# Decode attention: differential keys transposed by the vector engine in 32x32 blocks and fetched by GpSimd gathers

## The chip, the cores and the metric

The kernel runs on one core of one Trainium2 chip. The metric is the device time of one execution in microseconds (us). The engines are named as in the profile: PE (TensorE, matmuls), DVE (VectorE), ACT (ScalarE), POOL (GpSimd) and SP (SyncE, which here only issues DMAs). A change of 0.2% or more (3.4 us) is what a measurement of this kernel can tell from none.

## The reference, cut to what matters

One decoder layer is computed for a prompt of 512 tokens and for 8 sequences that decode 4 tokens each over 1024 cached tokens. The cache lies in pages of 128 tokens; a page table gives the 8 pages of each sequence. The change touches only the differential attention of the decoding sequences:

```
s_diff = cache_diff_kv[l][page_table].reshape(DB, past_len, 2, DIFF_HEADS, DIFF_DV)
s1 = einsum('bqhd,bkhd->bhqk', q1, k1) * scale + bias      # 8 heads, 64 dims
s2 = einsum('bqhd,bkhd->bhqk', q2, k2) * scale + bias      # the second half of each head
a  = masked_softmax(s1, mask) - lam * masked_softmax(s2, mask)
o  = einsum('bqhk,bkhd->bqhd', a, v)
```

A token has 1024 numbers of keys (8 heads, 2 halves, 64 dims) and 1024 of values, all float32.

## The kernel before, in words

The program has five stages: projections, compression, prompt attention, decode attention, and the closing stage (output projection and MLP). The change lies in decode attention, which runs from about 965 to 1237 us.

Decode attention takes two sequences at a time, in four pairs (i = 0 to 3). `decode_steps` writes the work of all pairs as one list of steps: `cmp` (compressed keys), `sel` (keys of 8 selected-branch pages), `win` (4 window blocks), `dif_n` and `dif` (the new rows and the 8 pages of differential keys, four steps each, m = 0 to 3), then `p_sel`, `p_few`, `p_win` (probabilities times values of the first three branches, "the value steps"), and `p_dif`, `p_dif_n` (probabilities times differential values), which stand in the middle of the next pair, after its sixth `sel` step. Before the change the value steps come after `dif` pages 0 and 1, in the last pair after page 7.

A step has two parts. `turn` makes PE transpose four 128x128 blocks into a PSUM bank, ACT or DVE copies the bank to a slot in SBUF (`owner` says which), and `multiply` makes PE multiply the slot with the queries. PE runs `turn` two steps ahead of `multiply`, and there are four banks and slots. So a page of differential keys costs 16 transposes, 4 copies of 128x512 and 16 score matmuls.

All engines work through the list in order and wait on semaphores. All page loads of this stage are issued by SP, in one order written by hand (`load_v` for differential values, 2 x 512 KB a page for the two sequences; `load_k`/`key_load` for differential keys, the same size; `sel_load`, 2 x 256 KB a page; `win_load`, 2 x 256 KB a block). A load waits for its buffer: values of page k for the `p_dif` matmuls of the pair before; a key page for the turns of the page four before it (there are four key buffers, `KEY_PAGES`); the selected pages of the next pair for all value steps of this one (`nsa_mm`). Key page 0, the selected pages and the windows of pair 0 are loaded during prompt attention.

The compression stage already fetches rows by GpSimd gathers (`page_rows`, L229: 128 rows of 2 KB by an indirect DMA).

## Time and profile before

| | |
|---|---|
| median of 3 runs | 1718.29 us (1717.81 to 1719.01) |
| the profiled execution: its time, its span | 1718.2 us, 1716.4 us |
| mean granted TensorE clock over the span | 0.967 |
| busy, share of the span | PE 93%, DVE 47%, ACT 33%, POOL 11% |
| DMA | 265.67 MB, 155 GB/s in the mean |
| the decode stage | 965.6 us (first DMA issue) to 1236.7 us (its last stores are issued) |

Spans and times of single instructions are from the one profiled execution; 1.8 us of its time lie outside its span. A PE that is shown busy need not be at its peak, and the time of a stage is set by whatever wait ends last in it, not by the busiest engine of the whole span.

### The profile page before, as it was taken

The page shows a single profiled execution, that of the slowest core. Times are in us where ns is not written, and L with a number is a line of the kernel's source. Part 1 is how long each engine was busy: PE and PEld are TensorE (multiplying, and loading weights), DVE is VectorE, ACT ScalarE, POOL GpSimd, SP SyncE. Part 2 cuts the span into 40 slices and gives each one's busy share as a digit, 9 for nine tenths or more (in the row PEclk, how much of TensorE's full clock was granted, in tenths as well). Part 3 has the DMA queues.
Part 4 walks back from the last instruction along what each step waited for, and adds up shares of the span by engine and source line. Part 5 has one row for each costly group of instructions (what it writes and reads, how often), then busy time and mean ns, then how long its engine had stood idle before and what let it go on. Part 6 is the DMA issues. An engine that isn't in the chain of part 4 may idle for free. (4 is left out here: it accounts for less than half of the span.)

```text
span 1716.4 us, 31637 instructions
## 1 busy us (share of the span) xinstructions
PE 1603.7 (93%) x12648; PEld 1329.8 (77%) x12648; DVE 808.1 (47%) x1841; ACT 570.8 (33%) x1185; POOL 180.4 (11%) x269
## 2 busy tenths in 40 slices
PE   6999999998999988799899899889799999999997
PEld 4878888876888875577777776666488999999996
DVE  4576632215443428776766545445355442234322
ACT  4233220223323226656555233233233331133210
POOL 2001000000630000073212000000000000000000
PEclk9999999999999998999999899999899999999998
DMA  8855443434631316344121499998542334334321
GB/s 272 308 172 170 165 139 141 144 84 102 183 105 28 105 38 183 84 173 138 44 77 38 169 386 369 370 347 294 220 143 89 123 103 117 122 99 135 84 73 53
DMA packets 184201, 265.67 MB, mean 155 GB/s; under 512 B 35661, under 2 KB 115917, under 8 KB 183958
## 3 DMA queue, kind: packets, MB, share of 16 engines
q1 hardware_dynamic: 174934, 227.57, 40.4%
q0 software_dynamic: 6016, 25.34, 4.9%
q10 hardware_dynamic: 3136, 11.22, 1.7%
q8 instruction: 73, 1.20, 0.3%
q14 instruction: 42, 0.34, 0.1%
HBM read 241.01 MB, written 42.60 MB: 165 GB/s over the span
## 5 line engine op out<-in xcount | busy, mean ns | idle before, releaser
L648 PE MATMUL pj_ps<-all_hi,pj_xh 128*128 128x512 f32 x480 | 191.7, 399 | 1.5 <-DVE all_lo L536 1.5
L649 PE MATMUL pj_ps<-all_lo,pj_xh 128*128 128x512 f32 x480 | 190.0, 396 | 0.0
L650 PE MATMUL pj_ps<-all_hi,pj_xl 128*128 128x512 f32 x480 | 189.9, 396 | 0.0
L1427 ACT ACTIVATE pa_sc<-pa_sc,pa_nmax 128x32 f32<-128x32 f32 (+4 forms) x256 | 126.0, 493 | 115.7 <-DVE pa_nmax L1476 115.5
L2685 PE MATMUL fi_ps<-fi_fl,fi_wh 128*128 128x272 f32 x512 | 149.2, 291 | 0.0
L2686 PE MATMUL fi_ps<-fi_fh,fi_wl 128*128 128x272 f32 x512 | 148.4, 290 | 0.0
L2684 PE MATMUL fi_ps<-fi_fh,fi_wh 128*128 128x272 f32 x512 | 148.3, 290 | 0.0
L2686 PE MATMUL fi_ps<-fi_th,fi_wl 128*128 128x272 f32 x512 | 148.3, 290 | 0.0
L2684 PE MATMUL fi_ps<-fi_th,fi_wh 128*128 128x272 f32 x512 | 147.6, 288 | 0.7 <-DVE fi_tl L2486 0.7
L2685 PE MATMUL fi_ps<-fi_tl,fi_wh 128*128 128x272 f32 x512 | 147.2, 287 | 0.0
L2069 ACT ACTIVATE de_slot<-de_ps_t 128x512 f32<-128x512 f32 (+5 forms) x124 | 62.8, 513 | 175.3 <-PE de_ps_t L1903 85.6
L2181 DVE COPY de_slot<-de_ps_t 128x512 f32<-128x512 f32 (+4 forms) x112 | 68.9, 623 | 104.8 <-PE de_ps_t L1903 59.0
L648 PEld LDWEIGHTS pj_ps<-all_hi,pj_xh 128*128 128x128 f32 x480 | 90.3, 188 | 26.3 <-issue 3.0
L1390 PE MATMUL pa_ps_t<-all_ident,pa_sc 128*128 128x128 f32 (+1 forms) x464 | 77.9, 286 | 34.7 <-DVE pa_keys L1484 12.1
L650 PEld LDWEIGHTS pj_ps<-all_hi,pj_xl 128*128 128x128 f32 x480 | 90.3, 188 | 21.9
L649 PEld LDWEIGHTS pj_ps<-all_lo,pj_xh 128*128 128x128 f32 x480 | 90.3, 188 | 21.0
L1024 PE MATMUL cm_ph<-cm_xh,all_hi 128*128 128x512 f32 x256 | 102.8, 402 | 2.3 <-DVE cm_xl L917 2.3
L2412 ACT ACTIVATE fi_wh<-all_big 128x2048 fp32r<-128x2048 f32 x30 | 57.3, 1908 | 138.5 <-PE fi_ps L2686 138.5
L1025 PE MATMUL cm_ph<-cm_xl,all_hi 128*128 128x512 f32 x256 | 101.9, 398 | 0.0
L1026 PE MATMUL cm_ph<-cm_xh,all_lo 128*128 128x512 f32 x256 | 101.8, 398 | 0.0
L2684 PEld LDWEIGHTS fi_ps<-fi_fh,fi_wh 128*128 128x128 f32 x512 | 97.2, 190 | 0.0
L2686 PEld LDWEIGHTS fi_ps<-fi_fh,fi_wl 128*128 128x128 f32 x512 | 97.1, 190 | 0.0
(328 smaller groups left out, 3175.3 us busy)
## 6 DMA issues: line engine op xcount, KB each, us to landing
de_dv<-in_cache_diff SPq DMA_DIRECT2D x64, 512.0 KB, 9.7
all_big<-in_w_in SPq DMA_DIRECT2D x14, 2048.0 KB, 10.1
de_dk<-in_cache_diff SPq DMA_DIRECT2D x48, 512.0 KB, 8.7
all_big<-in_cache_nsa SPq DMA_DIRECT2D x64, 256.0 KB, 6.4
all_big<-in_w_up SPq DMA_DIRECT2D x16, 1024.0 KB, 5.6
all_big<-in_w_down SPq DMA_DIRECT2D x16, 1024.0 KB, 5.5
all_win<-in_cache_win SPq DMA_DIRECT2D x32, 256.0 KB, 7.9
all_dk<-in_cache_diff SPq DMA_DIRECT2D x16, 512.0 KB, 8.7
```

The costliest lines, as they stand in the source:

```text
L648: pe.matmul(ps[:, t, :], xh[:, k, xk], hi(k), start=k == 0, stop=False)
L649: pe.matmul(ps[:, t, :], xh[:, k, xk], lo(k), start=False, stop=False)
L650: ins = pe.matmul(ps[:, t, :], xl[:, k, xk], hi(k), start=False, stop=k == KT - 1)
L1024: pe.matmul(o, w1h[k][:, kt, col], mh, start=first, stop=False)
L1025: pe.matmul(o, w1h[k][:, kt, col], ml, start=False, stop=False)
L1026: ins = pe.matmul(o, w1l[k][:, kt, col], mh, start=False, stop=last)
L1390: ins = pe.transpose(bank[0:r, P * k:P * (k + 1)], sc[:, x.n % 6, a, P * k:P * k + r], ident[:])
L1427: nc.scalar.activation(tile, tile, ACT.Exp, scale=-1.0, bias=nmax[:, x.n % 6, a:a + 1], accum_out=x.sums[a]).then_inc(probs, 1)
L2181: ins = nc.vector.tensor_copy(slot[rows, g % 4, cols], ps_t[rows, g % 4, cols])
L2684: pe.matmul(o, hi[:, k, :], a_hi[:, k, tok], start=k == 0, stop=False)
L2685: pe.matmul(o, hi[:, k, :], a_lo[:, k, tok], start=False, stop=False)
L2686: return pe.matmul(o, lo[:, k, :], a_hi[:, k, tok], start=False, stop=k == n_k - 1)
```

## The change

Differential keys are no longer transposed by PE. They are loaded in another layout: partition 64 b + 32 c + j holds of sequence b the tokens j, 32 + j, 64 + j, 96 + j (q = 0 to 3), of each the half c of its 1024 key numbers. One DVE instruction (`turn_keys`) then transposes the tile of 128x2048 in place, by 32x32 blocks; after it the partitions run over (b, c, 32 dims) and PE multiplies straight from the tile. The queries are loaded in a block layout too (`qd_rows`, `load_diff_rows`), and transposed by DVE, with no part of PE; so are the keys of the new tokens (`dk_n`).

The key pages 0 to 3 of pair 0 are still loaded by the hardware queue (`key_load`, now 4 DMAs of 256 KB a page). The other 28 pages are fetched by GpSimd, four gathers of 128 rows x 2 KB each (`gather_keys`). Their row numbers are computed on GpSimd in the first stage. The value steps of pairs 0 to 2 now stand after `dif` page 3 (`KEYS_FIRST` = 4), and `p_sel`, `p_few` and `p_win` are all copied by ACT.

```diff
 def key_load(sp, d, g, pages, i, k):
     n = (N_PAGES * i + k) % KEY_PAGES
+    keys = d["cache_diff"].rearrange("n (q j) e -> n j q e", j=32)
     for b in range(2):
-        sp.dma_start(g.ahead.dk[n][:, b, :], d["cache_diff"][bass.ds(pages[b][k], 1), :, 0:1024]
-                     .rearrange("n p e -> (n p) e")).then_inc(g.dk_in[n], 16)
+        for c in range(2):
+            at = 64 * b + 32 * c
+            sp.dma_start(key_tile(g.ahead.dk[n])[at:at + 32, :, :], keys[bass.ds(pages[b][k], 1), :, :, CW * c:CW * (c + 1)]
+                         .rearrange("n j q e -> (n j) q e")).then_inc(g.dk_in[n], 16)
...
-KEYS_FIRST = 2
+KEYS_FIRST = 4
...
-        Q_STEP = {AT[i - 1, "p_win", 0, 0] + 14: i for i in range(1, PAIRS)}
+        Q_STEP = {AT[i - 1, "p_win", 0, 0] + 6: i for i in range(1, PAIRS)}
...
+        def keys_free(n):
+            i, k = divmod(n, N_PAGES)
+            return (scores_mm, NG * i + GROUP_OF["dif", k] + 1) if k % 4 == 3 else (keys_read, 6 * i + k - k // 4 + 1)
+        KEYS_AT = {max(AT[i, "dif", k, 0] - 4, AT[i, "dif_n", 0, 0] if k < KEY_PAGES else 0): [] for i in pairs for k in range(N_PAGES)}
...
+            def load_diff_rows(i):
+                for b in range(2):
+                    at = 2 * DEC_T * i + DEC_T * b
+                    for c in range(2):
+                        cols = slice(CW * c, CW * (c + 1))
+                        rows = 64 * b + 32 * c
+                        sp.dma_start(dk_n[rows:rows + DEC_T, :], d["diff_s"][at:at + DEC_T, cols]).then_inc(dk_n_in, 16)
+                        for m in range(2):
+                            row = rows + 16 * b + 8 * m + 4 * c
+                            part_of = lambda ap: ap.rearrange("t (h m e) -> t h m e", h=4, m=2)[:, :, m, :]
+                            sp.dma_start(part_of(qd_rows[row:row + DEC_T, :]),
+                                         part_of(d["qd"][SEQ + at:SEQ + at + DEC_T, cols])).then_inc(dq_in, 16)
...
             load_new(0)
             for k in range(KEYS_AHEAD, KEY_PAGES):
-                load_k(shared.pages[0], 0, k)
+                key_load(sp, d, shared, shared.pages[0], 0, k)
+            sp.wait_ge(rows_zeroed, 2)
+            load_diff_rows(0)
             load_new_v(0)
...
-                for k in range(6):
+                for k in range(N_PAGES):
                     load_v(pages, i, k)
-                load_k(pages, i, 4)
-                load_v(pages, i, 6)
-                load_k(pages, i, 5)
-                load_v(pages, i, 7)
                 load_dv_new(i)
                 sp.wait_ge(nsa_mm, i + 1)
                 sel_load(sp, d, shared, following, range(0, 3))
                 load_new(i + 1)
-                load_k(pages, i, 6)
+                load_diff_rows(i + 1)
                 sel_load(sp, d, shared, following, range(3, 6))
                 load_new_v(i + 1)
-                load_k(pages, i, 7)
                 sel_load(sp, d, shared, following, range(6, 8))
                 win_load(sp, d, shared, i + 1)
-                for k in range(KEY_PAGES):
-                    load_k(following, i + 1, k)
...
         @block.gpsimd
         def _(pool):
+            def gather_keys(i, k):
+                n = N_PAGES * i + k
+                pool.wait_ge(*keys_free(n - KEY_PAGES))
+                for q in range(4):
+                    nc.gpsimd.indirect_dma_start(key_tile(dk[n % KEY_PAGES])[:, q, :], None, key_rows,
+                                                 bass.IndirectOffsetOnAxis(ap=shared.key_rows[:, n, q:q + 1], axis=0)
+                                                 ).then_inc(dk_got[n % KEY_PAGES], 16)
...
+                for k in (4, 5):
+                    gather_keys(i, k)
+                if i:
+                    pool.wait_ge(diff_out, i)
+                    for b in range(2):
+                        store_diff(pool, i - 1, b)
+                for k in (6, 7):
+                    gather_keys(i, k)
                 pool.wait_ge(nsa_out, i + 1)
...
                 if i + 1 < PAIRS:
+                    for k in range(KEY_PAGES):
+                        gather_keys(i + 1, k)
...
+                    for h in range(4):
+                        ins = pe.matmul(bank[32 * h:32 * h + 32, at:at + n], qdb[:, i % 2, 4 * h + m, :], keys[:, 4 * h + m, :, :],
+                                        start=m == 0, stop=m == 3)
...
             def lay_diff_queries(i):
...
+                dve.wait_ge(dq_in, 128 * i + 128)
+                nc.vector.transpose(qdb[:, i % 2, :, :].rearrange("p f c -> p (f c)"), qd_rows[:]).then_inc(qdb_ready, 1)
+
+            def turn_keys(i, k):
+                n = N_PAGES * i + k
+                if n < KEY_PAGES:
+                    dve.wait_ge(dk_in[n], 64)
+                else:
+                    dve.wait_ge(dk_got[n % KEY_PAGES], 64 * (n // KEY_PAGES))
+                tile = dk[n % KEY_PAGES][:].rearrange("p b e -> p (b e)")
+                nc.vector.transpose(tile, tile).then_inc(keys_turned, 1)
```

The rest of the diff builds the constants for the new layout: `b_dif` is loaded by 16 DMAs in place of 8, and GpSimd computes `key_rows` in the first stage.

On DVE, in pair 0, from the scaling of the softmax of the first branches to the last copy before pair 1 (`de_slot` is the slot of a step, `de_ps_t` the PSUM banks, `de_s_dif` the differential scores). Before:

```order
L2228 TENSOR_SCALAR de_cm<-all_ident,de_rr 128x128 x3
L2181 COPY de_slot<-de_ps_t 128x512 x2
L2181 COPY de_slot<-de_ps_t 4x256
L2181 COPY de_slot<-de_ps_t 64x64 x2
L2181 COPY de_slot<-de_ps_t 128x512 x2
L2237 TENSOR_TENSOR de_part<-de_ps_n,all_con 128x128
L2242 TENSOR_REDUCE de_o_n<-de_part 128x64
L2181 COPY de_slot<-de_ps_t 128x512 x4
L2095 ISA de_s_dif,de_nm<-de_ps_s,all_b_dif 128x512
```

And after the change, where `all_dk0`, `de_dk1` to `de_dk3` are the four key buffers:

```order
L2285 TENSOR_SCALAR de_cm<-all_ident,de_rr 128x128 x3
L2216 STREAM_TRANSPOSE de_dk2<-de_dk2 128x2048
L2216 STREAM_TRANSPOSE de_dk3<-de_dk3 128x2048
L2216 STREAM_TRANSPOSE all_dk0<-all_dk0 128x2048
L2144 ISA de_s_dif,de_nm<-de_ps_s,all_b_dif 128x512
L2144 ISA de_nm 128x1
L2216 STREAM_TRANSPOSE de_dk1<-de_dk1 128x2048
L2294 TENSOR_TENSOR de_part<-de_ps_n,all_con 128x128
L2299 TENSOR_REDUCE de_o_n<-de_part 128x64
L2216 STREAM_TRANSPOSE de_dk2<-de_dk2 128x2048
L2199 COPY de_qb<-de_ps_n 64x4x2x4 x4
L2207 STREAM_TRANSPOSE de_qdb<-de_qd_rows 128x512
```

The copies of the key steps are gone, and the transposes of key pages 2 to 6 stand in their place; page 7 follows, behind the transpose of the next pair's queries (L2207), which waits for `dq_in`.

On SP, behind the first three selected pages for pair 1 (`all_big` holds the selected pages, `de_new_rows` the new tokens' rows). Before:

```order
L197 DMA all_big<-in_cache_nsa 128x512
L1771 DMA de_new_rows<-out_nsa_s 4x2x512
L1772 DMA de_new_rows<-out_win_s 4x2x512
L1774 DMA de_new_rows<-out_diff_s 4x2x1024
L210 REGISTER_ALU
L210 DMA de_dk<-in_cache_diff 128x1024
```

After:

```order
L194 ISA
L194 DMA all_big<-in_cache_nsa 128x512
L1803 DMA de_new_rows<-out_nsa_s 4x2x512
L1804 DMA de_new_rows<-out_win_s 4x2x512
L1814 DMA de_dk_n<-out_diff_s 4x512
L1818 DMA de_qd_rows<-scratch_qd 4x4x64 x2
```

The last two rows stand four times in a row, so twelve small DMAs take the place of one; the key page that followed is gone from this queue. The queries of the next pair, which were loaded ahead of the values (L184), are now loaded behind them and behind three selected pages.

## Rows read from the trace of the kernel before

**Rows 1.** Busy us by stretch: PE, PEld, DVE, ACT, POOL; clock; DMA share; GB/s.
```profile
965.00:1212.00 247.00, 232.19 (x3340) 171.05 (x3341) 119.00 (x333) 80.42 (x158) 10.06 (x18) 0.93 0.96 352
```

**Rows 2.** The same view, stretches of 4 us in decode.
```profile
996.00:1000.00 4.00, 4.00 (x96) 3.15 (x88) 1.01 (x3) 0.60 (x1) 0.00 (x0) 1.00 1.02 410
...
1016.00:1020.00 4.00, 4.00 (x42) 2.77 (x40) 1.38 (x2) 0.60 (x1) 0.00 (x0) 0.50 1.05 387
...
1036.00:1040.00 4.00, 4.00 (x40) 1.17 (x36) 0.55 (x1) 0.02 (x1) 0.00 (x0) 1.00 0.87 304
...
1084.00:1088.00 4.00, 1.44 (x7) 1.44 (x8) 0.00 (x0) 0.28 (x1) 0.00 (x0) 0.77 1.04 383
...
1184.00:1188.00 4.00, 3.34 (x35) 2.58 (x36) 3.07 (x13) 2.21 (x5) 0.00 (x0) 0.65 0.10 22
```

**Rows 3.** Waits in decode: who waited for whom, us in total, times, longest.
```profile
SPq L210 <- PE de_ps_t L1903: 49.0, 13, 11.4
...
PEld de_ps_t L1903 <- DMA de_dk<-in_cache_diff: 11.5, 5, 4.7
```

**Rows 4.** Timeline of PE in decode: start, us, instructions.
```profile
987.94 0.42 PE L1960 MATMUL de_ps_s<-de_slot,de_qdb 128*32 128x128 f32 x8 [0.25 <-DVE de_slot L2181]
...
1035.75 6.64 PE L2000 MATMUL de_ps_d<-de_dv,de_slot 128*32 128x512 f32 x60
...
1100.50 7.05 PE L2000 MATMUL de_ps_d<-de_dv,de_slot 128*32 128x512 f32 x64
...
1168.98 7.07 PE L2000 MATMUL de_ps_d<-de_dv,de_slot 128*32 128x512 f32 x64
...
1189.59 1.09 PE L1903 MATMUL de_ps_t<-all_ident,de_dk 128*128 128x128 f32 x8
1190.61 0.64 PE L1960 MATMUL de_ps_s<-de_slot,de_qdb 128*32 128x128 f32 x16
```

**Rows 5.** Timeline of SP's queue: issue start, us of issuing, DMAs.
```profile
703.67 0.34 SPq L185 DMA_DIRECT2D all_kc<-scratch_kc_s  x1
733.83 9.07 SPq L197 DMA_DIRECT2D all_big<-in_cache_nsa  x16
...
966.31 0.29 SPq L1774 DMA_DIRECT2D de_new_rows<-out_diff_s  x1
966.81 3.23 SPq L210 DMA_DIRECT2D de_dk<-in_cache_diff  x6
...
1002.43 3.25 SPq L197 DMA_DIRECT2D all_big<-in_cache_nsa  x6
```

**Rows 6.** Timeline of POOL: gathers for the compression stage.
```profile
106.86 1.21 POOL L229 DMA_INDIRECT all_first<-in_cache_nsa,all_row_ids  x1 [66.72 <-PE pj_ps L639]
...
441.88 0.95 POOL L229 DMA_INDIRECT all_big<-in_cache_nsa,all_row_ids  x1 [0.30 <-issue]
```

**Rows 7.** DMA in two stretches: gathers by queue and time to landing; 2 KB rows of SP.
```profile
q0 software_dynamic: 1856, 6.10, 68.1%
...
all_big<-in_cache_nsa,all_row_ids POOLq DMA_INDIRECT x9, 3.6
...
742.00:748.00 6.00, 5.89 (x30) 3.27 (x30) 4.81 (x14) 3.13 (x10) 5.45 (x8) 0.76 1.04 394
```

**Rows 8.** DVE: the first slot copy of decode, and two groups by shape.
```profile
971.10 0.17 DVE L2181 COPY de_slot<-de_ps_t 128x16 f32<-128x16 f32 x1
...
L2181 DVE COPY de_slot<-de_ps_t 128x512 f32<-128x512 f32 x95 | 64.9, 690 | 93.2 <-PE de_ps_t L1903 59.0 <-PE de_ps_t L1880 27.4 <-PE de_ps_t L1911 5.3
...
L2577 DVE TENSOR_TENSOR fi_wl<-all_big,fi_wh 128x2048 fp32r<-128x2048 f32 x30 | 68.8, 2293 | 30.7 <-ACT fi_wh L2412 30.7
```

**Rows 9.** Timeline of the end of decode.
```profile
1210.38 2.05 PE L1911 MATMUL de_ps_t<-de_cm,de_s_sel 128*128 128x128 f32 x16
...
1220.61 1.08 PE L1990 MATMUL de_ps_n<-de_new_rows,de_slot 4*32 4x128 f32 x16
...
1236.73 1.54 SPq L1763 DMA_DIRECT2D scratch_ob<-de_o_d  x2
```

More of the change, by code:

```diff
@@ L159 @@
 KEY_PAGES, KEYS_AHEAD = 4, 1
-N_CONSTS = 14
+N_CONSTS = 22
 def constant_loads(sp, d, g):
@@ L492, in _ @@
             pool.wait_ge(shared.ids_in, 16 * 2)
+            numbers = shared.page_ids[:].rearrange("p (i b k) -> p i b k", b=2, k=N_PAGES)
+            for b in range(2):
+                step(nc.gpsimd.tensor_scalar(own[:, b, :].rearrange("p (i k) -> p i k", k=N_PAGES), numbers[:, :, b, :],
+                                             place[:, 12 + b:13 + b], None, ALU.mult))
+            step(nc.gpsimd.tensor_tensor(own[:, 0, :], own[:, 0, :], own[:, 1, :], ALU.add))
+            for q in range(4):
+                nc.gpsimd.tensor_scalar(shared.key_rows[:, :, q], own[:, 0, :], place[:, 8 + q:9 + q], None, ALU.add
+                                        ).then_inc(shared.key_ids_ready, 1)
+            pool.wait_ge(shared.key_ids_ready, 4)
+            own = own[:, :, 0:2 * N_PAGES]
             for x in range(4):
@@ L1812, in _ @@
                 sp.wait_ge(q_turned, i + 1)
-                sp.wait_ge(turned, AT[i, "cmp", 0, 0] + 1)
+                sp.wait_ge(turned, turns[AT[i, "cmp", 0, 0]])
                 pair_rows(sp, d, shared, i + 1)
-                for k in range(6):
+                for k in range(N_PAGES):
                     load_v(pages, i, k)
-                load_k(pages, i, 4)
-                load_v(pages, i, 6)
-                load_k(pages, i, 5)
-                load_v(pages, i, 7)
                 load_dv_new(i)
@@ L1959, in multiply @@
                                 c = P * x + CMPS * b
-                            ins = pe.matmul(bank[rows, at:at + n], lhs, tile[:, c:c + n], start=m == 0,
-                                            stop=m == 3 or kind not in ("dif", "dif_n"))
-                    if kind == "win_n" or (kind == "dif_n" and m == 3):
+                            ins = pe.matmul(bank[rows, at:at + n], qb[:, x, b, :], tile[:, c:c + n], start=True, stop=True)
+                    if kind == "win_n":
                         ins.then_inc(few_mm, 1)
@@ L2020, in turn_queries @@
                     half, at = slice(DK * (g % 2), DK * (g % 2 + 1)), Q_AT + 32 * (g // 2) + 8 * h
-                    pe.matmul(ps_n[half, at:at + 8], qn[:, DK * x:DK * (x + 1)], ident[0:2 * DEC_T, 0:2 * DEC_T],
-                              start=True, stop=True)
-                one = slice(32, 32 + 2 * DEC_T)
-                for h in range(DHEADS):
-                    at = Q_AT + 64 + 8 * h
-                    ins = pe.transpose(ps_n[:, at:at + 8], qd[:, P * h:P * (h + 1)], ident[one, one])
+                    ins = pe.matmul(ps_n[half, at:at + 8], qn[:, DK * x:DK * (x + 1)], ident[0:2 * DEC_T, 0:2 * DEC_T],
+                                    start=True, stop=True)
                 ins.then_inc(q_turned, 1)
@@ L2178, in _ @@
                 if g < N and owner[g] == "dve":
-                    dve.wait_ge(turned, g + 1)
+                    dve.wait_ge(turned, turns[g])
                     for rows, cols in pieces(g):
-                        ins = nc.vector.tensor_copy(slot[rows, g % 4, cols], ps_t[rows, g % 4, cols])
+                        ins = nc.vector.tensor_copy(slot[rows, ring[g], cols], ps_t[rows, ring[g], cols])
                     ins.then_inc(copied["dve"], 1)
+                if g < N and STEPS[g][1:] == ("dif_n", 0, 0):
+                    dve.wait_ge(dk_n_in, 64 * STEPS[g][0] + 64)
+                    nc.vector.transpose(dk_n[:], dk_n[:]).then_inc(dk_n_turned, 1)
+                for i, k in KEYS_AT.get(g, ()):
+                    turn_keys(i, k)
                 if g in READ_AT:
```

165 lines of the change are left out of this document (80 added, 85 removed).

## The prediction

> **What bounds the kernel now.** The page's busy shares name PE, but they average over five stages, and the change touches only decode, so that stage was read by stretches. From 965 to 1212 us PE is busy 232 of 247 us, and the DMA engines 96% at 352 GB/s [rows 1]. Both are nearly full. In stretches of 4 us the DMA runs at 410 GB/s where 4 KB rows flow and at 387 with 2 KB rows; it falls to 304 where the values of a pair begin, and to 22 at 1184 us, in the last pair [rows 2]. The waits say why: SP waited 49 us in 13 pieces for PE's transposes before it could issue key pages, and PE waited 11.5 us for key pages [rows 3]. PE and the loads hold each other up. At full flow a page of keys or values (two sequences, 1.05 MB) takes 2.66 us, by the 394 GB/s of 2 KB rows [rows 7].
>
> A pair moves 8 pages of keys, 8 of values, 4 page sizes of selected pages and 2 of windows: 22, or 58.5 us. The `p_dif` matmuls, which free the value pages, begin at 1035.8, 1100.5 and 1169.0 us [rows 4]. I call these points P1, P2 and P3; pairs are 64.7 and 68.5 us apart. The last key step is done at 1210.4, and the last stores are issued at 1236.7 [rows 9]. So 6 to 10 us of a pair are above the pure transfer time. That is the most a relief of PE can give: it cannot give the PE work itself.
>
> **What the change removes.** PE loses 16 transposes a page, 2.18 us (twice the 1.09 us of 8), and keeps 16 score matmuls, 0.64 us [rows 4]: 70 us over 32 pages. Almost none of it comes off the end directly, since the DMA lies under it. Of the 128 copies of the key steps DVE loses about half, 0.69 us each [rows 8], 11 us a pair. The queries' DMA ahead of the values goes too.
>
> **What it adds.**
> 1. DVE turns a page in one instruction of 128x2048. No row shows this operation. The nearest is another pass of DVE over 128x2048 float32, 2.29 us [rows 8]; I take 2.3. Below it the bound is 2.14, the 1.04 ns an element between this row and the 0.69 us of a 128x512 copy, with no fixed part; above it 4.6, twice the row, if the instruction needs two passes. Eight turns are 18.4 us a pair for 11 us of copies; DVE is busy 119 of 247 us [rows 1], so it has room, but pages 0 to 3 stand one behind the other and PE waits for each.
> The Trainium skill ("VectorE: DVE Perf Modes", section The three transpose paths) gives 311 ns for the 32x32 transposes of one 128x128 tile; an estimate from it for the 16 such tiles of a page is 5.0 us, and by it the sum would be 1731. No run here shows it yet.
> 2. A gather of 256 KB takes POOL 0.95 us and the next comes 1.25 us after it, landing after 3.6 us [rows 6, 7]. A page is 5.0 us of POOL, so this queue moves at most 210 GB/s. Beside it SP's queue keeps about 184 of 394 GB/s, 5.7 us a page size.
> 3. Twelve small DMAs on SP in place of one, about 0.29 us each [rows 5]: 3.5 us of issuing a pair. The page loads issued ahead cover it, as far as they are there; I charge 1 to 2 us of transfer a pair (the 304 GB/s stretch is what small loads and an emptied queue do).
> 4. Eight more constant loads on SP, some 4 us of issuing, lie in its wait from 704 to 733.8 us [rows 5], and GpSimd's row numbers in the 66.7 us that it waits before its first gather [rows 6]. They cost nothing; without that cover they would cost what they take, 4 us and a few more.
>
> **New waits.** (a) At the start DVE transposes the queries before its first copy. They are loaded behind 12 key DMAs, 6.5 us of issuing at the 3.23 us of 6 [rows 5], and 12 small ones, 3.5 to 4 us, and land near 979.6. DVE's first copy stood at 971.1 [rows 8]: 8.5 us later, and PE can run only a few steps ahead of it. (b) In each pair DVE must turn the next pair's queries before key page 7 (L2207 ahead of the next L2216). They land behind all values of the pair and 1.5 page sizes of selected pages. Behind that wait stand page 7, the last scores, and the next pair's copies. (c) The value steps stand behind key pages 0 to 3, so `nsa_mm`, which lets SP go on to the next pair's pages, comes later in the pair.
>
> **The sum, by points.** *P1.* The first differential score stood at 987.9 [rows 4] and moves to 996. Three more turns and the scaling, 9 us, and 8.8 us of value steps put `nsa_mm` at 1014; it was at 1002.4 [rows 5]. SP has nothing to load from 1001.5 (3 and 8 pages) to 1014. Then three page sizes beside the gathers, 17 us, 3 for small loads, 2 for landing, and two steps: P1 is at 1037.6, 1.8 later than before, with 3 page sizes of this pair still queued.
> *P2.* Those take until 1046.6. PE reads key page 0 at P1 + 15.5 (7.1 for `p_dif` [rows 4], 1.1 for its new rows, 5.2 for the last six steps of selected pages and windows at 1.09 + 0.64 for two, 2.3 for the turn) and POOL begins to fetch. By then 2.5 pages of values are in; 5.5 x 5.7 = 31 us bring the rest, to 1084. The 1.5 page sizes and the small rows end at 1093, page 7 is turned at 1096. Its scores, the exponentials, and six steps take 9 us: P2 at 1105.6, 5.1 later.
> *P3.* Less is queued now (0.6 of a page size). The queries land at 1151.6, page 7 is turned at 1154, P3 is at 1163.6, 5.4 earlier than before: 126 us for the two pairs instead of 133.
> *The end.* PE reads key page 0 at P3 + 15.5 = 1179. POOL issues four pages in 20 us, the last lands 3 us later, 2.3 for the turn, 0.65 for the scores: 1205.1, against 1210.4. From there to the stores it was 26.3 us [rows 9] and the order is the same. But PE now waits 4 us of every 5 before it. After a stretch with 1.44 of 4 us busy the granted clock was 0.77, and at 1016 it was 0.50, the lower level of 1.2 GHz [rows 2]. In the end of decode 16 matmuls into 32 partitions took 1.08 us, where 16 took 0.64 in the last pair's key steps [rows 4, 9]. I charge 2.5 us for one more such spell.
> Together -5.3 + 2.5 = -2.8 us. The profiled execution took 1718.2 us, so the sum is 1715.4, and since it stands 0.1 below the median, 1715.
>
> **The rivals.**
> *The flow is better than I charge (0.22).* Two queues keep the engines supplied, and the falls to 304 and 22 GB/s go. For it: full stretches reach 410 [rows 2]. Against it: nothing here shows both queues at once in full flow. At 2.56 us a page size a pair takes 58 us plus 1 to 2: 3 us less a pair, about 1704.
> *Gathered bytes cost the DMA engines more (0.16), the case on the other side.* The gathers moved 6.10 MB in 30 us at 68.1% [rows 7], 298 GB/s per full share, against 394. Then a page costs 3.5 us and not 2.66, 28 pages 24 us, of which some 18 fall where the DMA is full: 1733. Against it: the queue was never backed up there. It decides from 0.1 us a page on, which is all the gain of 2.8 us.
> *The turn takes 4.6 us (0.10).* The first pair's chain is 4 x 2.3 longer and the last pair's 2 x 2.3; the pairs between have cover: +14 us, 1729. It loses from about 2.8 us a turn on.
> *The waits for the queries weigh more (0.10).* If wait (b) is not caught up in the third pair as it is in my P3, each pair keeps its 3 to 4 us, and a clock of 0.50 stretches the chain to the next `p_dif`: +8, 1723.
> *My forecast (0.42)*: 1715, its own range 1708 to 1722.
>
> **How the numbers follow.** What can be told from no change is 0.2%, 3.4 us: 1714.9 to 1721.7. Of the 0.42 I give 0.20 to faster, 0.18 to the same, 0.04 to slower; the better flow is faster, the gathers and the turn slower, the waits 0.02 the same and 0.08 slower. That is 0.42 faster, 0.20 the same, 0.38 slower. The range must leave out no more than 2 in 10: 1702 takes in the better flow, 1732 the slow turn and nearly half of the costly gathers.
>
> **What would show it.** The profile after should have gathers 1.25 us apart, L2216 at 2.3 us with 32 of them, no L1903 transposes, DVE's first copy near 979.6, SP's first selected pages near 1014, `p_dif` near 1037.6, 1105.6 and 1163.6, and the decode stage's last stores near 1234. A DVE wait on `de_qd_rows` ahead of page 7 of some us a pair confirms (b). Gathers more than 1.4 us apart, a turn above 3 us, or full stretches under 370 GB/s would make me wrong on the slow side; a mean above 370 GB/s from 965 to 1200 on the fast side.

## The result and the profile after

The changed kernel takes 1763.7 us in the median (1755.2 to 1765.6, 4 runs), the kernel before beside it 1718.05 us (1716.9 to 1719.0): a ratio of 1.0256, 95% interval 1.022 to 1.029. The forecast of 1715 us was 49 us too low, and its range did not hold the time.

The page of the profiled execution (1765.6 us):

```profile
span 1763.4 us, 30330 instructions
PE 1553.4 (88%) x12040; PEld 1293.3 (73%) x12040; DVE 832.6 (47%) x1788; ACT 536.5 (30%) x1119; POOL 289.2 (16%) x388
q1 hardware_dynamic: 168582, 198.21, 35.3%
q0 software_dynamic: 14976, 54.71, 9.6%
```

PE did lose its transposes, and the keys did move to GpSimd's queue. Decode by stretches, each from one `p_dif` point to the next, the last to the last stores (us, then PE, PEld, DVE, ACT, POOL busy, clock, DMA share, GB/s); first the changed kernel:

```profile
968.55:1060.00 91.45, 52.72 (x816) 41.03 (x817) 41.62 (x91) 13.08 (x29) 31.57 (x34) 0.68 0.89 287
1060.00:1132.00 72.00, 47.60 (x740) 33.49 (x742) 37.03 (x72) 13.15 (x26) 33.90 (x38) 0.74 0.92 327
1132.00:1207.00 75.00, 50.06 (x763) 34.43 (x766) 37.75 (x76) 13.55 (x26) 33.94 (x38) 0.75 0.92 326
1207.00:1287.00 80.00, 51.16 (x668) 30.28 (x668) 34.65 (x61) 12.04 (x21) 18.70 (x22) 0.70 0.59 214
```

and the same stretches of the kernel before:

```profile
965.60:1036.00 70.40, 68.45 (x984) 54.09 (x988) 35.51 (x108) 22.21 (x46) 1.15 (x2) 0.87 1.00 370
1036.00:1100.00 64.00, 58.53 (x881) 42.67 (x874) 30.17 (x85) 20.95 (x43) 3.33 (x6) 0.97 1.01 370
1100.00:1169.00 69.00, 63.12 (x917) 45.22 (x914) 31.68 (x90) 22.05 (x42) 3.31 (x6) 0.95 0.97 356
1169.00:1237.00 68.00, 61.87 (x813) 39.77 (x812) 28.38 (x71) 20.68 (x38) 3.31 (x6) 0.92 0.70 252
```

In the mean over a pair nothing is full any more: PE is busy 53 of 91 us and 48 of 72, and the flow fell from 370 to 327 GB/s. PE's busy time in decode fell by 50.4 us (252.0 to 201.5), not by the 70 us of the transposes taken away; the granted clock fell from 0.87 to 0.97 before to 0.68 to 0.75, and the work that was left ran longer.

Where the time went is read from points of the timelines: the first DMA issue of decode, SP's first load of the next selected pages (`nsa_mm`), the first `p_dif` matmul (P), the last stores. In us between them:

| | start to nsa_mm | to P1 | P1 to nsa_mm | to P2 | P2 to nsa_mm | to P3 | P3 to stores | sum |
|---|---|---|---|---|---|---|---|---|
| before | 36.8 | 33.3 | 30.1 | 34.7 | 32.7 | 35.8 | 67.8 | 271.1 |
| changed | 60.2 | 31.8 | 41.0 | 30.6 | 42.0 | 32.8 | 79.7 | 318.0 |
| difference | +23.4 | -1.5 | +10.9 | -4.1 | +9.3 | -3.0 | +11.9 | +46.9 |

**The start.** DVE's first rows, then SP's:

```profile
990.10 0.71 DVE L2207 STREAM_TRANSPOSE de_qdb<-de_qd_rows 128x512 f32<-128x512 f32 x1 [18.06 <-DMA de_qd_rows<-scratch_qd]
991.14 0.77 DVE L2233 COPY de_slot<-de_ps_t 128x16 f32<-128x16 f32 x2
```
```profile
969.42 6.31 SPq L211 DMA_DIRECT2D de_dk<-in_cache_diff  x12
1028.76 3.39 SPq L194 DMA_DIRECT2D all_big<-in_cache_nsa  x6
```

The first copy, at 971.10 before [rows 8], stands behind the transposed queries and comes at 991.14. The flow in that time, in stretches of 4 us:

```profile
973.00:977.00 4.00, 1.10 (x12) 0.53 (x10) 0.00 (x0) 0.00 (x0) 0.00 (x0) 0.50 1.03 205
977.00:981.00 4.00, 0.00 (x0) 0.00 (x0) 0.00 (x0) 0.00 (x0) 0.00 (x0) 0.50 1.07 214
```

All 16 engines are shown busy and move 205 to 214 GB/s, where 4 KB rows into 128 partitions moved 410 [rows 2]. The key loads of 32 partitions run at half the rate, with the queries behind them. The 2 KB rows alone are not the reason: rows of 2 KB into 128 partitions moved 394 [rows 7].

**A pair.** DVE's turns of the second pair, then POOL's first gather of page 4:

```profile
1075.73 2.27 DVE L2216 STREAM_TRANSPOSE all_dk<-all_dk 128x2048 f32<-128x2048 f32 x1
1078.70 2.30 DVE L2216 STREAM_TRANSPOSE de_dk<-de_dk 128x2048 f32<-128x2048 f32 x1
1082.81 2.31 DVE L2216 STREAM_TRANSPOSE de_dk<-de_dk 128x2048 f32<-128x2048 f32 x1
1087.64 2.30 DVE L2216 STREAM_TRANSPOSE de_dk<-de_dk 128x2048 f32<-128x2048 f32 x1
1091.56 2.31 DVE L2216 STREAM_TRANSPOSE all_dk<-all_dk 128x2048 f32<-128x2048 f32 x1 [1.18 <-DMA all_dk<-in_cache_diff,all_key_rows]
1096.62 2.31 DVE L2216 STREAM_TRANSPOSE de_dk<-de_dk 128x2048 f32<-128x2048 f32 x1
1116.30 0.71 DVE L2207 STREAM_TRANSPOSE de_qdb<-de_qd_rows 128x512 f32<-128x512 f32 x1 [10.95 <-DMA de_qd_rows<-scratch_qd]
```
```profile
1080.38 0.94 POOL L1884 DMA_INDIRECT all_dk<-in_cache_diff,all_key_rows  x1 [25.38 <-PE de_ps_s L1986]
```

Pages 0 to 3 have long landed, yet they are turned from 1075.7 to 1089.9, one behind the other with reads and the output's scaling between. Only when page 0 is scored does POOL, idle for 25.4 us, fetch page 4. Then page 7 waits for the queries. PE's waits from P1 to `nsa_mm` (1060.56 to 1101.58; total, times, longest), first the changed kernel, then the kernel before (1035.75 to 1065.84):

```profile
PE de_ps_s L1986 <- DVE de_dk L2216: 6.0, 3, 2.9
PE de_ps_n L1986 <- DVE de_dk_n L2237: 3.2, 1, 3.2
PE de_ps_s L1986 <- DVE all_dk L2216: 1.6, 1, 1.6
```
```profile
PE de_ps_n L1960 <- DVE de_slot L2181: 0.9, 1, 0.9
```

So 7.6 us are waits for the four turned pages, and 3.2 us are for the pair's new keys, which DVE transposes (L2237) behind its choice of the selected blocks. From `nsa_mm` to P2 it is another matter: there the DMA is full, as it was before (a share of 1.02 from 1065.8 to 1100.5 us), and the loads that `nsa_mm` releases set the time.

```profile
1101.60:1132.00 30.40, 16.81 (x276) 13.24 (x272) 12.18 (x30) 5.32 (x11) 17.55 (x20) 0.72 0.99 351
```

What SP waited for `nsa_mm` in the three pairs, before and after:

```profile
SPq L197 <- PE de_ps_n L1975: 22.0, 3, 7.3
```
```profile
SPq L194 <- PE de_ps_n L2028: 85.7, 3, 31.4
```

The waits of the whole stage (total, times, longest):

```profile
POOL all_dk L1884 <- PE de_ps_s L1986: 123.2, 4, 46.7
PE de_ps_s L1986 <- DVE de_dk L2216: 74.0, 19, 14.1
DVE de_qdb L2207 <- DMA de_qd_rows<-scratch_qd: 50.8, 4, 18.1
```

### The profile page after: what moved, and what is told of

It is laid out like the page before. It is cut to its first block and busy times, and to the rows that moved or that the text cites. A ratio compares the mean times of both kernels' runs of the same rounds, so it can differ in the third digit from the quotient of the medians.

```text
span 1763.4 us, 30330 instructions
## 1 busy us (share of the span) xinstructions
PE 1553.4 (88%) x12040; PEld 1293.3 (73%) x12040; DVE 832.6 (47%) x1788; ACT 536.5 (30%) x1119; POOL 289.2 (16%) x388
## 5 line engine op out<-in xcount | busy, mean ns | idle before, releaser
L1405 PE MATMUL pa_ps_t<-all_ident,pa_sc 128*128 128x128 f32 (+1 forms) x464 | 80.1, 292 | 35.4 <-DVE pa_keys L1499 11.9
L1986 PE MATMUL de_ps_s<-de_dk,de_qdb 128*32 128x128 f32 x768 | 43.2, 378 | 74.2 <-DVE de_dk L2216 74.0
L2741 PEld LDWEIGHTS fi_ps<-fi_th,fi_wh 128*128 128x128 f32 x512 | 96.4, 188 | 0.8 <-DVE fi_tl L2543 0.8
L2742 PEld LDWEIGHTS fi_ps<-fi_tl,fi_wh 128*128 128x128 f32 x512 | 96.5, 189 | 0.0
## 6 DMA issues: line engine op xcount, KB each, us to landing
all_win<-in_cache_win SPq DMA_DIRECT2D x32, 256.0 KB, 10.6
```

Of the source, the lines that this page charges most:

```text
L1405: ins = pe.transpose(bank[0:r, P * k:P * (k + 1)], sc[:, x.n % 6, a, P * k:P * k + r], ident[:])
L2741: pe.matmul(o, hi[:, k, :], a_hi[:, k, tok], start=k == 0, stop=False)
L2742: pe.matmul(o, hi[:, k, :], a_lo[:, k, tok], start=False, stop=False)
```

## The experiments

A total also holds the stages ahead of decode, in which nothing was edited: decode started between 956.0 and 968.7 us in e1 to e4 and g1 to g4. So edits are compared by the table's stretches, each from one profiled execution. How far one execution can be trusted is seen where the same program was run again (e7, f2 and h1; e6, f1 and h2, below): the sums agree within 2 and 5 us, so a difference of 3 us between two sums says nothing. The runs c1, e5 to e8, f1 to f3, h1 and h2 were made on other chips, where the kernel before took 1742 to 1745 us, and are compared among themselves (c1).

**Single repairs.** e1, the order at the start:

```diff
             load_new(0)
+            sp.wait_ge(rows_zeroed, 2)
+            load_diff_rows(0)
             for k in range(KEYS_AHEAD, KEY_PAGES):
                 key_load(sp, d, shared, shared.pages[0], 0, k)
-            sp.wait_ge(rows_zeroed, 2)
-            load_diff_rows(0)
```

> One thing is moved: at the start of decode SP issues the 12 small rows (queries and new keys of pair 0) ahead of the 12 loads of key pages 1 to 3. Theory L (the late queries hold the start): they landed at 990 us, and DVE waited 18.1 us for them. Issued first they land near 977, DVE's first copy goes from 991.1 to about 978, the first differential score from 1009.1 to about 998, and the time falls by 8 to 13 us, to about 1753. Rival F (the key loads' own slow flow, 211 GB/s from 975 to 985, holds the start): the keys land 4 us later than now, and the time falls by less than 3 us.

e2, the queries of the next pair early:

```diff
                 pair_rows(sp, d, shared, i + 1)
+                sp.wait_ge(qdb_ready, i + 1)
+                load_diff_rows(i + 1, keys=False)
...
-                load_diff_rows(i + 1)
+                load_diff_rows(i + 1, queries=False)
```

> The 8 small loads of the next pair's queries are issued with its nsa query rows, ahead of the values, and not after the first selected pages; the new keys' 4 loads stay. Theory L: DVE's waits for these rows ahead of key page 7 (10.2, 11.0 and about 11.6 us) go, page 7 follows page 6 by its gather alone (5 us of POOL, of which some is hidden), and each of the three p_dif points comes 6 to 9 us earlier than without: in all -18 to -27 us, about 1741. Rival G (the gathers of pages 4 to 7, 5 us each, and the turns set the pair's length anyway): the wait passes to the landing of page 7, and the time falls by less than 6 us.

e3 is `KEYS_FIRST = 2` for 4:

> The value steps of pairs 0 to 2 stand behind key pages 0 and 1, as in the kernel before, and not behind 0 to 3. Theory L: nsa_mm and with it the next selected pages and query rows come about 5 us earlier in each pair (two turns of 2.3 us), so the queries' wait shrinks by as much, and the time falls by 6 to 12 us, to about 1755. Rival V (the value steps' place is of no weight, or they delay pages 2 and 3 and with them POOL's gathers of pages 6 and 7 as much as they gain): within 3 us of 1764.

e4, pages 1 to 3 of pair 0 by gathers (`key_load` for them is gone from SP):

```diff
             pool.wait_ge(shared.key_ids_ready, 4)
+            for k in range(KEYS_AHEAD, KEY_PAGES):
+                gather_keys(0, k)
```

> Key pages 1 to 3 of pair 0 are fetched by 12 gathers of GpSimd at the start of decode in place of 12 queue loads of 32 partitions each; SP then issues the 12 small rows at once. Theory L: the queries land near 977 as with the rows first, the last of the 12 gathers near 969 + 15 + 3 = 987, the first differential score near 998, and the time is that of the rows-first kernel within 3 us, about 1753. Rival F (the loads of 32 partitions are slow by their form): the gathers let the selected pages' and values' flow be fuller, and the time is 3 us or more below the rows-first kernel.

| | ratio to before | start to nsa_mm | to P1 | P1 to nsa_mm | to P2 | P3 to stores | sum |
|---|---|---|---|---|---|---|---|
| changed | 1.0256 | 60.2 | 31.8 | 41.0 | 30.6 | 79.7 | 318.0 |
| e1 | 1.0183 (1.013 to 1.023) | 43.7 | 45.6 | 40.7 | 32.8 | 79.3 | 318.2 |
| e2 | 1.0178 (1.012 to 1.024) | 59.7 | 31.8 | 41.2 | 30.4 | 79.9 | 317.6 |
| e3 | 1.0218 (1.015 to 1.029) | 55.1 | 38.1 | 33.2 | 36.6 | 79.5 | 315.0 |
| e4 | 1.0158 (1.010 to 1.022) | 46.5 | 31.7 | 41.1 | 32.4 | 73.1 | 298.8 |

In the table of the result and in this one, "changed" and e1 to e4 have times of 1763.7, 1753.3, 1755.2, 1754.8 and 1750.7 us. Most of these differences are not the edits': e1 came out at the 1753 that was expected of theory L, but its decode stage is as long as the changed kernel's (318.2 against 318.0 us) and only began 12 us earlier. That hit was luck.

e1 brings `nsa_mm` forward by 16.5 us and loses 13.8 of them in the next stretch; the start is held by the late queries, as theory L says, but the gain is not kept. DVE's rows of e1 say to what:

```profile
1006.96 2.31 DVE L2216 STREAM_TRANSPOSE de_dk<-de_dk 128x2048 f32<-128x2048 f32 x1 [2.60 <-DMA de_dk<-in_cache_diff,all_key_rows]
1029.12 0.71 DVE L2207 STREAM_TRANSPOSE de_qdb<-de_qd_rows 128x512 f32<-128x512 f32 x1 [19.17 <-DMA de_qd_rows<-scratch_qd]
```

The key loads, still at half rate, and the values behind them now ran into the gathers, and the next queries landed 19 us after DVE wanted them. With the slow loads gone as well (e4) the 13.7 us gained stay, and the stage is 19.4 us shorter than e1's, as rival F says and not theory L (the times differ by 2.6 us only, since e4's decode began 12 us later). e4's last stretch is shorter too, by 6.6 us, though no edit touches it: its last 13 us ran at a clock of 0.94, the changed kernel's last 20 at 0.82, and PE was busy 46.8 us in the stretch against 51.2. That stretch can't be read finer.

e2 is a miss that taught most. The wait of 10 to 12 us for the queries is gone, and the pair is as long as it was. PE's rows of e2 ahead of P2:

```profile
1106.19 1.08 PE L1989 MATMUL de_ps_s<-de_dk,de_qdb 128*32 128x128 f32 x16 [4.06 <-DVE de_dk L2219]
1116.75 0.71 PE L1927 MATMUL de_ps_t<-all_ident,all_big 128*128 128x128 f32 x4 [1.73 <-DMA all_big<-in_cache_nsa]
1126.50 1.94 PE L2056 MATMUL de_ps_d<-de_dv,de_slot 128*32 128x512 f32 x12
```

Page 7 is scored 51.3 us after P1 (1106.2 after 1054.9), against 58.7 in the changed kernel, but P2 stands behind six selected pages, which are only issued from `nsa_mm` on. From there to P took 33 to 36 us before the change too. So the longest wait of a pair cost nothing: what grew is the way from P to `nsa_mm`. e3 shortens that way by 8 us and lengthens the other by 6; its sum, 3 us less, can't be told from no gain. It says what the 8 us are: of the 10.9 us by which P1 to `nsa_mm` had grown, most are pages 2 and 3, which `KEYS_FIRST = 4` puts ahead of the value steps.

**The repairs together, on two other chips.** e5 is e4, e2, e3 together and POOL's gathers of pages 6 and 7 ahead of its stores; e6 and f1 are e5 with

```diff
+        for i in pairs[1:]:
+            for k in (0, 1, 2):
+                [v.remove((i, k)) for v in KEYS_AT.values() if (i, k) in v]
+                KEYS_AT.setdefault(AT[i - 1, "p_dif_n", 0, 0], []).append((i, k))
```

e7 and f2 turn a sixteenth of a page (the scores are of unturned keys):

```diff
-                nc.vector.transpose(tile, tile).then_inc(keys_turned, 1)
+                nc.vector.transpose(tile[:, 0:32], tile[:, 0:32]).then_inc(keys_turned, 1)
```

e8 splits a key load over q and not over c (8 DMAs of 64 partitions x 512); f3 gives the second column half of the 12 loads to ACT's queue; c1 is the changed kernel.

> Four edits together: key pages 1 to 3 of pair 0 by gathers, the next pair's query rows ahead of its values' loads, the value steps behind key pages 0 and 1, and POOL's gathers of pages 6 and 7 ahead of its stores of the pair before. Taken from the runs of the single parts: each part only uncovered the next wait (with early queries a pair kept its 72 us, because page 7 was then held by its gather). Theory C (the chain of a pair is p_dif to page 0, 15.6 us; pages 0 to 7, 33 us, set by gathers that start at page 0's scores; page 7 to the next p_dif, 22.7 us): together they take about 14 us off the start and 2.4 us of stores off each of three pairs, and the last stores stand at about 290 us from the start of decode (318.0 before these edits); total about 1737. Rival D (the DMA flow binds once the waits are gone): the pairs stay at 71 to 73 us and the total is about 1750, as with the first pages by gather alone.

> The kernel of the four edits, and DVE turns key pages 0 to 2 of pairs 1 to 3 in its idle 8 us under p_dif, ahead of the last selected pages, and not behind the pair's new keys. Theory C: page 0's scores still come 15.6 us after p_dif begins, but pages 0 to 2 then follow at 0.65 us each, POOL's gathers find their slots free at once, and each of three pairs gets 3 to 7 us shorter: 9 to 20 us below the four edits. Rival D (the gathers, 5 us a page from page 0's scores on, already end later than the turns): within 4 us of the four edits.

> The changed kernel with each key page's turn cut to one instruction of 128x32, so that only a sixteenth of the page is turned; the differential scores are therefore of unturned keys. It prices DVE's turns on the path: 32 x 2.2 us of DVE work are gone. Theory C (late queries, gathers and flow carry most of the loss): 4 serial turns at the start and 2 or 3 at the end of the chain, 12 to 18 us less, about 1748, still well above the kernel before. Rival T (the turns, serial in front of PE, are the loss): three or four turns in every pair and the cold clock behind them, 30 us or more less, about 1730 or under.

> The changed kernel with each queue-loaded key page (page 0, and 1 to 3 of pair 0) in 8 DMAs of 64 partitions x 512 elements instead of 4 of 32 partitions x 2048. Bytes and row size (2 KB) are the same. Theory W (the few partitions at a time are what slows the flow to 211 GB/s): the stretch in which they land shows clearly more, 300 GB/s or above. Rival R (something else, the 2 KB rows or the queue itself): 200 to 230 GB/s again. The total is not of use for this, since SP issues 12 more DMAs ahead of the queries, about 6 us.

> The changed kernel itself, unedited, as the base for the others of this call: the chip of the last call ran the kernel before at 1742.7 us and not 1718, and the matmuls of decode were issued up to 5 us late there without any wait that the profile shows, so those runs can only be read against a changed kernel on the same chip. Expected: a ratio of 1.022 to 1.030 to the kernel before, as in the first result, if the loss is the kernel's and not the chip's.

> The kernel of the four edits (first pages by gather, early queries, values behind pages 0 and 1, stores behind the gathers) with pages 0 to 2 turned under p_dif, beside its own base this time. Theory C (a pair is the sum of three serial stretches: p_dif to page 0, the eight pages at the rate of the gathers, page 7 to the next p_dif): 14 us less at the start and 5 to 9 less in each of three pairs, a ratio of 1.003 to 1.010 to the kernel before. Rival D (the flow of the DMA binds as soon as the waits are gone): the pairs keep their 71 to 73 us and the ratio is 1.016 or more, as with the first pages by gather alone.

> The changed kernel with each page's turn cut to 128x32 (scores of unturned keys), beside its own base. Theory C: 12 to 18 us below the changed kernel, that is what four serial turns at the start and two or three at the end cost; the pairs between keep 70 us or more. Rival T (the turns are the loss): 30 us or more below it.

> The changed kernel with the 12 loads of 32 partitions at the start of decode shared out: the 6 of the first column half from SP as before, the 6 of the second half from ACT's queue at the same time, so that two groups of 32 partitions are written at once. Theory W (32 partitions written by all 16 engines at once set the 211 GB/s): 300 GB/s or above in the stretch in which they land, the queries land 4 to 7 us earlier. Rival R (the rate is of the reads, or of the engines on such rows): 200 to 230 GB/s as before, and the queries land at most 1 to 3 us earlier, by the shorter issue alone.

| | ratio to before | start to nsa_mm | to P1 | P1 to nsa_mm | P3 to stores | sum |
|---|---|---|---|---|---|---|
| c1 | 1.0394 (1.036 to 1.043) | 68.8 | 33.4 | 49.8 | 79.7 | 350.2 |
| e5 | 1.0406 (1.035 to 1.046) | 52.8 | 46.9 | 37.4 | 76.5 | 342.8 |
| e6, f1 | 1.0355, 1.0326 | 52.8 | 47.0, 46.4 | 33.7, 33.9 | 73.8, 69.1 | 336.0, 331.2 |
| e7, f2 | 1.0327, 1.0320 | 67.4, 67.6 | 31.9 | 46.6, 44.6 | 67.1, 69.4 | 327.2, 328.2 |
| f3 | one execution | 60.5 | 32.6 | 50.0 | 74.9 | 333.5 |

c1 missed: decode is 32 us longer here with the same program. PE's waits in c1 name it, first of the compression stage, then of decode:

```profile
PE cm_ph L1040 <- issue: 7.4, 6, 2.0
```
```profile
PE de_ps_s L1986 <- issue: 28.2, 18, 7.0
PE de_ps_n L2028 <- issue: 9.6, 14, 1.1
```

Matmuls were issued late for no wait that the profile shows. Between 560 and 985 us, where no gathers run, there is none of this, and in decode some 40 of 43.6 us of it lie beside a gather (the timelines of PE and POOL laid over each other), though gathers are being issued in only 140 of the 350 us. In the first result's trace the same two stages show no such wait. What delays the issue was not found.

The short turn takes 22 to 23 us off: more than theory C's 12 to 18 and less than rival T's 30. PE's waits for turned pages between P1 and `nsa_mm` are then gone (5.7 us in c1), but that stretch is only 3 to 5 us shorter. The four edits of e5 give 7 us and no better ratio than c1; with the early turns of e6 and f1 it is 14 and 19 of 350 us, about what e4 gave alone. P1 to `nsa_mm` falls by 12 to 16 us and `nsa_mm` to P grows by nearly as much. Theory C's gains did not add up; rival D names the size, and its cause, a full flow, is shown for the changed kernel behind `nsa_mm` but not here.

e8 tells nothing of W, since its loads ran on few engines: SP's queue and the flow of e8:

```profile
994.13 56.08 SPq L210 DMA_DIRECT2D de_dk<-in_cache_diff  x24
```
```profile
1007.00:1011.00 4.00, 0.00 (x0) 0.00 (x0) 0.00 (x0) 0.00 (x0) 0.00 (x0) 0.50 0.13 49
```

A share of 0.13 is 2 of 16 engines, and the outermost dimension of that pattern is 2. The Trainium skill (DMA: Bandwidth & Descriptors, section Why a DMA increments its semaphore by 16 and not by 1) says that the number of engines is the largest up to 16 that divides the slowest dimension of both sides; the trace agrees.

f3's flow stayed as it was, first with SP's loads, then with ACT's:

```profile
1001.00:1005.00 4.00, 0.00 (x0) 0.00 (x0) 0.00 (x0) 0.00 (x0) 0.00 (x0) 0.50 1.01 214
1005.00:1009.00 4.00, 0.44 (x8) 0.23 (x8) 0.43 (x1) 0.46 (x2) 0.00 (x0) 0.50 0.93 199
```

But this is no test of W either, since the two halves were not written at once:

```profile
996.20 2.83 SPq L211 DMA_DIRECT2D de_dk<-in_cache_diff  x6
1004.24 3.17 ACTq L211 DMA_DIRECT2D de_dk<-in_cache_diff  x6
```

ACT issued its six loads 8 us after SP had begun with its own, and six loads take 7.5 us at 210 GB/s. What of these loads halves the rate stays open. The Trainium skill (SBUF — State Buffer, section Door 1: The DMA port swizzle) says that 32 partitions reach 8 of the 16 ports of SBUF, and the 32 next to them reach the same 8. By it half the rate is due to each of these loads. The trace agrees in the size (205 to 214 against 402 to 412 GB/s); no run wrote two such groups together. The queries landed 7.8 us earlier in f3, more than R's 1 to 3, since half of the slow loads no longer stood ahead of them.

**Half gathers and short turns, where matmuls are not issued late.** g1 leaves out half of each gathered page (`range(2)` for `range(4)`, so half of its keys are stale), g3 does that and the short turn (scores of unturned and stale keys), g2 is e6 with pages 5 and 7 by SP (`key_load` behind the values and behind the first selected pages), g4 is the kernel before with `KEYS_FIRST = 4`.

> The changed kernel with two of the four gathers of every gathered key page left out (half of its keys are stale, so the differential scores are not the reference's). Theory C (the gathers' 5 us a page, from page 0's scores to page 7, are one of the three serial stretches of a pair): pages 4 to 7 take 10 us of POOL and not 20, the pairs shorten by 4 to 8 us each where the queries' wait does not take their place, the last pair, which has no such wait, by about 10, and the time falls by 15 to 30 us. Rival Q (the queries' wait ahead of page 7 then holds the first three pairs as before): only the last pair gains, about 10 us. Rival F (bytes on the DMA engines bind): 29 pages' halves, 15 MB at 390 GB/s, 39 us less.

> The four edits and the early turns, and key pages 5 and 7 of each pair by SP's queue, so that POOL fetches two and SP two of the pages that a pair waits for. Theory C: pages 4 to 7 are there about 10 us earlier after page 0's scores, each pair shortens by some 5 us against the early turns, and the time comes to the kernel before's within 0.5%. Rival F (the slow flow of queue loads of 32 partitions, 205 to 214 GB/s at a full share of the engines, costs what POOL's time saves): no better than the early turns alone.

> Half the gathers and a turn of 128x32 at once (scores not the reference's). Theory C: both stretches are serial, so their gains add: that of half the gathers and 12 to 18 us more. Rival: one of the two hides behind the other, and this kernel is within 4 us of half the gathers alone.

> The kernel before the change with one number of it changed: the value steps behind key pages 0 to 3 and not 0 and 1. It shows what that part of the change costs by itself, where PE turns the keys. Theory L: nsa_mm comes about 14 us later in a pair (8 steps of 1.73 us), and SP, which then waits for it with nothing else to load, loses 4 to 8 us of flow in each of three pairs: 1.007 to 1.013 of the kernel before. Rival V (the place is of no weight): within 0.3%.

| | ratio to before | start to nsa_mm | to P1 | P1 to nsa_mm | to P2 | P2 to nsa_mm | P3 to stores | sum |
|---|---|---|---|---|---|---|---|---|
| g1 | 1.0198 (1.012 to 1.027) | 58.7 | 30.8 | 41.3 | 30.0 | 42.3 | 72.5 | 305.9 |
| g3 | 0.9960 (0.993 to 0.999) | 52.3 | 27.9 | 30.7 | 28.6 | 32.0 | 59.0 | 259.2 |
| g2 | 1.0232 (1.020 to 1.027) | 43.3 | 44.3 | 27.2 | 50.2 | 30.2 | 71.1 | 305.9 |
| g4 | 1.0175 (1.014 to 1.021) | 43.1 | 39.4 | 37.2 | 37.0 | 39.5 | 63.8 | 299.7 |

g1 rules out that bytes or the rate of the gathers set a pair by themselves: with half of both, P1 to `nsa_mm` stays 41 us. Most of its gain, 7.2 of 12.1 us, is in the last stretch, where PE's waits for turned pages fall from 17.7 to 11.2 us; that is what rival Q says, not theory C. g3 takes P to `nsa_mm` from 41.0 to 30.7 and from 42.0 to 32.0 us, all that the change had added, 7.9 us off the start and 20.7 off the end, 59 us in all. From g1 to g3 only the turn differs: 46.7 us, of which 6.4 at the start, 10.6 and 10.3 from P to `nsa_mm`, 13.5 at the end. PE's waits from P1 to `nsa_mm` in g3, where the changed kernel and g1 both have 10.8 us:

```profile
PE de_ps_n L1986 <- DVE de_dk_n L2237: 3.2, 1, 3.2
PE de_ps_s L1986 <- DVE de_dk L2216: 0.6, 1, 0.6
```

Its stretches:

```profile
966.30:1047.00 80.70, 50.52 (x824) 40.81 (x828) 25.32 (x92) 13.66 (x30) 16.49 (x18) 0.71 0.88 283
1047.00:1106.00 59.00, 44.55 (x742) 32.50 (x738) 20.67 (x73) 12.55 (x25) 18.84 (x22) 0.80 0.93 330
1167.00:1226.00 59.00, 42.46 (x668) 26.15 (x660) 17.62 (x61) 11.85 (x20) 11.18 (x14) 0.87 0.68 252
```

After the start the clock is back at 0.80 to 0.87. g3's decode is 12 us shorter than that of the kernel before; that is no price of PE's relief alone, since g3 also leaves out 14.7 MB of keys, 37 us of transfer at 394 GB/s. g2 only moves the wait: `nsa_mm` to P grows to 44 and 50 us, with page 7 now behind SP's loads. g4 costs the kernel before 28.6 us of decode and 1.75% of its time, more than the 0.7 to 1.3% that I expected; its PE waits 30.9 us for keys that SP brings late, against 9.9 without the edit:

```profile
PE de_ps_t L1903 <- DMA de_dk<-in_cache_diff: 30.9, 6, 8.7
```

**The short turn alone and all repairs together,** again on a chip where matmuls are issued late:

> The turn of 128x32 alone (scores of unturned keys), to complete the table of four: whole gathers and whole turns 318.0 us from the start of decode to its last stores, half gathers 305.9, both cut 259.2. On the chip where matmuls are issued late it took 21.6 us off. If turn and gather stand in series in the loop through a page buffer (gathered, turned, scored, free again), each cut alone leaves the other and the wait for the queries, and this one gives 295 to 303 us, a ratio near 1.013. If the turns were the loss by themselves, as rival T has it, it gives 275 us or less, a ratio near 1.00.

> The four edits and the early turns (output as the reference's), for the size of the repair where matmuls are not issued late. From the first pages by gather alone (298.8 us to the last stores) and 5 to 9 us for the pairs: 285 to 292 us, a ratio of 1.007 to 1.013; the kernel before stays faster, since the gathers' 5 us a page are still in the loop. Rival D (the flow binds): 298 us or more, 1.016 or more.

They gave 1.0324 (1.025 to 1.040; decode 328.9) and 1.0352 (1.027 to 1.043; 332.2), as e7 and f2, and e6 and f1. So on a chip without late matmuls the short turn alone stays unmeasured, and how g3's 59 us divide stays open: half gathers alone are 12, a short turn alone 21 to 23 on the other chips, a short turn on top of half gathers 47, more than these two together suggest. No version that computes everything beat the kernel before; the best, e4, is 1.6% slower.

## Why the prediction was wrong

- **Turn, 2.3 us**: right, 2.29 and 2.30 us. The rival of 4.6 us is refuted, and "No row shows this operation" was wrong: the kernel before has the operation at half the width, in its compression stage,

```profile
L894 DVE STREAM_TRANSPOSE all_laid<-all_big 128x1024 f32<-128x1024 f32 x8 | 9.5, 1223 | 9.0 <-DMA all_big<-in_cache_nsa,all_row_ids 8.7
```

  which gives at most 2.45 us a page and would have ruled the rival out. The 5.0 us, 16 times the 311 ns that the Trainium skill (VectorE: DVE Perf Modes, section The three transpose paths) has for one 128x128 tile in bf16, are refuted as well. The trace does not contradict the 311 ns: from 0.70 us for 128x512 and 2.30 for 128x2048 I estimate 0.17 us fixed and 1.04 ns an element, 0.30 us for one tile alone. The step that failed is taking the fixed part 16 times.
- **Gathers**: 0.95 us and 1.25 apart, right. **Small DMAs**: 12 in 3.9 us, right. **Constants**: no cost can be seen (decode began at 968.6, and in seven more kernels with the same code ahead of it between 956.0 and 968.7).
- **Wait (a), the queries "land near 979.6"**: the first step that failed. First copy 991.1. I took the issue time of the 12 key DMAs and not their flow, and no row of before showed a load of 32 partitions. e1 and e4 show 14 to 16 us in it; the turns are another 6 us (g1 to g3), and I had counted 9 with the scaling. P1 was summed at 72.0 us from the start of decode and stood at 92.0.
- **P2 and P3 from the flow** (5.5 x 5.7 us): the second. The pairs took 71.6 and 74.8 us, the sum had 68.0 and 58.0. I counted four serial turns for pair 0 ("three more turns and the scaling") and for the others only those of pages 0 and 7, and let the transfers set the length as if SP never stopped. But P to `nsa_mm` grew by 10.9 and 9.3 us, and SP stood 85.7 us for `nsa_mm`, not 22.0. PE's waits in the first of these stretches are 10.8 us, 7.6 for the turned pages 0 to 3 and 3.2 for the new keys, a wait that is in no term of the sum and that no run removed. g1 and g3 show the turns' part by an edit: with the short turn the stretch is back at 30.7 us, with half gathers alone it is not.
- **Wait (b)**: there, 10.2 to 11.6 us against my 3 to 4, but e2 shows that it cost nothing: six selected pages behind `nsa_mm` cover it. The rival "the waits for the queries weigh more" had the sign by the wrong mechanism.
- **Wait (c)**: `nsa_mm(0)` at 1028.8 against 1014, late by (a). g4 shows that the place of the value steps costs 28.6 us where PE turns the keys; here e3 moves 8 us from one side of `nsa_mm` to the other and gains 3, which is not clear of nothing. I had a number for it in pair 0 (SP idle until 1014) and none for the other pairs.
- **The end**: P3 to the last stores 79.7 us against 70.4. Not by the clock on the last steps, for which I had charged 2.5 us: from the first score of page 7 it is 29.8 us against 29.5. POOL's first gather started 19.8 us after P3 and not 15.5, with the new keys' wait and PE at 0.50 in front of it. And its four pages took 24.8 us and not 20, since its stores of the pair before (L1795) stand between pages 5 and 6:

```profile
1237.05 1.79 POOL L1795 DMA_DIRECT2D scratch_ob<-de_o_d  x3 [0.61 <-DVE de_o_d L2318]
1241.75 1.02 POOL L1884 DMA_INDIRECT de_dk<-in_cache_diff,all_key_rows  x1 [0.30 <-issue]
```

  These two terms are the 9 us.
- **Better flow, costly gathers**: neither. Full stretches with both queues ran at 395 to 408 GB/s (e1, 981 to 1005 us), so gathered bytes cost what others do.

20.0 us of P1, 20.4 of the two pairs and 9.2 of the end make the 49.6 us by which the stage missed its sum. Of the sizes only the flow of the 12 key loads was wrong; the structure was wrong in the rest: I asked of each new operation whether its engine or the DMA had room, and not how many of them stand one behind the other between two points that release each other.

## What to carry to other kernels

An engine with half its time free can still add its whole duration: count how often the moved operation stands in series between the points that free a buffer and start a load, in every round and not just in the first. Check the longest wait by asking what else ends just after it; removing a wait of 11 us a pair gave nothing here, while waits of 1 to 3 us, one behind the other, made up the 10 us that `nsa_mm` came later. Relief of a busy PE is given back in part when it starts to wait: its clock in decode fell from 0.93 to 0.71 in the mean, and some 20 of 70 us of saved work came back as longer matmuls. Look for the new operation in every stage of the old trace before pricing it by something near.

## What the hardware showed that I had not expected

- Loads into 32 partitions ran at 205 to 214 GB/s with all engines shown busy, half of the 402 to 412 of loads into 128; a load whose outermost dimension was 2 used 2 engines, 49 GB/s.
- On the three chips of c1, e5 and h1 matmuls were issued up to 7 us late (up to 11 in f3), only in stages with GpSimd gathers, 32 to 63 us in decode; on the one where it was measured the change cost 3.9% and not 2.6%. In the first result, in e1 to e4 and in g1, g3 and g4 there is none of it.
- A turn of 128x2048 float32 in place by 32x32 blocks took 2.30 us, as much as another pass of DVE over as many elements [rows 8]; 128x1024 took 1.22, 128x512 0.70 and 128x32 0.20 us.
